# Seven of eight down-projection slices by one level of Strassen's algorithm, in a two-layer decoder step

## The reference, cut to what matters

```
def sqrelu_mlp(h, w_up, w_down):
    return jnp.square(jax.nn.relu(h @ w_up)) @ w_down

x += sqrelu_mlp(rms_norm(x, g), w_up, w_down)      # twice: layer 0 and layer 1
```

## Time and profile before

| | us |
|---|---|
| median of 3 runs | 2395.38 |
| lowest, highest run | 2393.91, 2808.45 |
| span of the profiled execution, first to last instruction | 2393.5 |

### The profile page before, as it was taken

One profiled execution on the slowest core, in us unless ns is written; L12 is line 12 of the kernel. 1 busy time (PEld: TensorE's weight loads), 2 busy tenths in 40 slices (PEclk: granted clock), 3 DMA queues, 4 the chain that ended last, 5 costly groups with the idle time before them and its releaser, 6 DMA issues.

```text
span 2393.5 us, 35212 instructions
## 1 busy us (share of the span) xinstructions
PE 2375.2 (99%) x15165; PEld 2312.2 (97%) x15165; DVE 1002.9 (42%) x1410; ACT 574.3 (24%) x1022; POOL 112.3 (5%) x131
## 2 busy tenths in 40 slices
PE   8999999999999999999999999999999999999999
PEld 8997899999999999999999998889999999999999
DVE  6449724433433333435623325545343333333333
ACT  6549722111111111102310115422111110110111
POOL 1005400000000000000000004100000000000000
PEclk9999999999999999999999999999999999999999
DMA  8621031111111111111321126341111111111112
GB/s 228 87 48 71 11 100 52 38 53 36 53 35 53 38 50 46 42 38 50 100 66 36 36 99 187 126 132 36 53 53 36 53 35 53 35 53 36 52 36 73
DMA packets 134264, 150.30 MB, mean 63 GB/s; under 512 B 33581, under 2 KB 109449, under 8 KB 134012
## 3 DMA queue, kind: packets, MB, share of 16 engines
q1 hardware_dynamic: 131228, 136.11, 19.2%
q0 software_dynamic: 2720, 12.56, 1.6%
q10 hardware_dynamic: 224, 0.30, 0.0%
HBM read 126.50 MB, written 24.47 MB: 63 GB/s over the span
## 4 chain that ended last, share of the span: by engine, by line
PE 96%; ACT 1%; DVE 1%; issue 0%; DMA 0%; DVEq 0%
PE ps L316 42%; PE ps L323 21%; PE ps L300 8%; PE ps L304 7%; PE ps L301 7%; PE ps L551 1%; PE ps L1033 1%; PE ps L1009 1%; PE ps L990 1%; ACT prob L1101 1%; PE ps L2080 1%; PE ps L1410 1%; PE ps L1411 1%; PE ps L1412 1%; PE ps L2061 1%; PE ps L2065 1%
## 5 line engine op out<-in xcount | busy, mean ns | idle before, releaser
L1537 DVE TENSOR_TENSOR x<-x,ps 128x1074 f32<-128x1074 f32 (+1 forms) x126 | 159.3, 1264 | 448.7 <-PE ps L323 448.7
L264 ACT ACTIVATE w_hi<-raw 128x1024 fp32r<-128x1024 f32 x180 | 187.4, 1050 | 648.8 <-PE ps L323 485.6
L316 PE MATMUL ps<-h_hi,w_lo 128*128 128x352 f32 (+2 forms) x1536 | 333.5, 325 | 0.0
L316 PE MATMUL ps<-h_hi,w_hi 128*128 128x352 f32 (+2 forms) x1536 | 333.4, 325 | 0.0
L316 PE MATMUL ps<-act_hi,w_hi 128*128 128x358 f32 (+1 forms) x1512 | 329.5, 326 | 0.0
L316 PE MATMUL ps<-act_hi,w_lo 128*128 128x358 f32 (+1 forms) x1512 | 328.5, 325 | 0.0
L323 PE MATMUL ps<-act_lo,w_hi 128*128 128x358 f32 (+1 forms) x1512 | 269.7, 325 | 0.0
L1519 DVE SCALAR_TENSOR_TENSOR relu<-ps,rstd 128x1074 f32<-128x1074 f32 (+1 forms) x64 | 81.1, 1267 | 447.4 <-PE ps L323 447.4
L316 PEld LDWEIGHTS ps<-h_hi,w_lo 128*128 128x128 f32 x1536 | 263.7, 189 | 0.0
L316 PEld LDWEIGHTS ps<-h_hi,w_hi 128*128 128x128 f32 x1536 | 263.5, 189 | 0.0
L323 PE MATMUL ps<-h_lo,w_hi 128*128 128x352 f32 (+2 forms) x1536 | 263.5, 326 | 0.0
(11 more groups left out here) (339 smaller groups left out, 2419.6 us busy)
## 6 DMA issues: line engine op xcount, KB each, us to landing
raw<-in_mlp_w_up SPq DMA_DIRECT2D x32, 1024.0 KB, 5.5
raw<-in_mlp_w_down SPq DMA_DIRECT2D x32, 1024.0 KB, 5.0
raw<-in_mlstm_w_in SPq DMA_DIRECT2D x12, 1024.0 KB, 5.4
x<-scratch_x SPq DMA_DIRECT2D x8, 537.0 KB, 6.2
scratch_x<-x POOLq DMA_DIRECT2D x1, 4296.0 KB, 14.1
x<-scratch_x SPq DMA_DIRECT2D x8, 528.0 KB, 4.7
x_tok<-in_x_prompt SPq DMA_DIRECT2D x8, 512.0 KB, 7.8
raw<-in_attn_w_qkv SPq DMA_DIRECT2D x16, 256.0 KB, 6.7
```

Of the source, the lines that this page charges most:

```text
L264: nc.scalar.activation(unit_view(w_hi, slot, down), raw_unit(j, rslot, down), ACT.Copy).then_inc(w_hi_ready, 1)
L316: nc.tensor.matmul(ps[:, bank + g, 0:c.stop - c.start], w_block(w, slot, k, kc, cols), hi[:, k, c], start=start and i == 0, stop=False)
L1537: nc.vector.tensor_tensor(view(x[:, o, :]), view(x[:, o, :]), ps[:, out_banks(n):out_banks(n) + 3, 0:w], ALU.add).then_inc(out_free, 1)
```

## The change

The first seven slices of each layer make the down-projection by one level of Strassen's algorithm. The eighth slice keeps the old way. The weights of a slice (512 hidden rows by 1024 outputs) are taken in 4 pairs `p` of output blocks, each pair a 2 x 2 matrix of halves: hidden half `kh` by output half `fh`. The activations of the slice are a 2 x 2 matrix too: hidden half by token half (536 columns, 528 in layer 1). Seven products P1 to P7 of (a weight or a sum of weights) with (an activation or a sum of activations) replace eight. A product has 2 x 2 x 3 = 12 matmuls of 268 (264) columns; 28 products make a slice.

The running sums are made in place: the activations' by `t_pool` and the weights' by `weight_sum_pool`, both on POOL. The partial sums that several outputs share stay in PSUM: chain "a" holds P1, then P1+P6, P1+P6+P5, and P1+P6+P5+P3, and after each step `add_dve` adds the content to one quarter of `x`. A product may only start when the add of the product before it in the chain is done (`earlier` in `product_pe`). 28 adds of 536 columns replace 8 of 1072.

Seven factors of 536 columns for each of two hidden blocks `idx` (14 in all) are split by `factor_hi` (ACT) and `factor_lo` (DVE), where 4 activations were split before. The weights of a product are 256 columns wide and are split by `prod_hi` and `prod_lo` into a ring of 11 slots, which the up blocks' weights share. POOL's order in a slice is: for `idx` 0 the sums t0 to t3; t0 of `idx` 1; the first weight sum; t1 to t3 of `idx` 1; then for each pair the weight sums 1, 2, 3 and sum 0 of the next pair. The up block called 4 in the new code is block 0 of the next slice, made ahead of the products; the last product runs behind the first step of the next up block. Weights come in DMAs of 512 KB instead of 1 MB. The small matrix `head_ones` leaves the first load of constants and comes by a DMA of its own, and several tiles move to other addresses.

```diff
+PRODUCTS = {"P1": (0, 0, 0, "a", True, 0, 0), "P7": (0, 1, 4, "b", True, 1, 1), "P6": (0, 1, 5, "a", False, 1, 0),
+            "P2": (1, 0, 2, "g", True, 0, 0), "P4": (1, 1, 6, "b", False, 1, 0), "P5": (0, 0, 1, "a", False, 1, 1),
+            "P3": (1, 0, 3, "a", False, 0, 1)}
+for _p in range(PAIRS):
+    ORDER += [("P1", _p)] + ([("P3", _p - 1)] if _p else []) + [(_n, _p) for _n in ("P7", "P6", "P2", "P4", "P5")]
+ORDER.append(("P3", PAIRS - 1))
+FACTORS = tuple((idx, f) for idx in range(2) for f in (0, 1, 3, 2, 4, 5, 6))
...
+        def product_pe(pe, layer, i, m):
+            name, p = ORDER[m]
+            _, _, f, chain, start, _, _ = PRODUCTS[name]
+            earlier = {"P6": ("P1", p), "P5": ("P6", p), "P3": ("P5", p), "P4": ("P7", p),
+                       "P7": ("P4", p - 1), "P2": ("P2", p - 1), "P1": ("P3", p - 2)}[name]
+            pe.wait_ge(ring_lo_ready, since("ring_lo_ready", layer, i * EVENTS + (E_M0 + m + 1)))
+            if earlier in M_OF:
+                pe.wait_ge(added, since("added", layer, i * NPROD + (M_OF[earlier] + 1)))
+            if m < 7:
+                pe.wait_ge(fac_lo, since("fac_lo", layer, i * NFAC + (FAC_OF[1, f] + 1)))
+            if m == 0:
+                pe.wait_ge(up_taken, since("up_taken", layer, i * 4 + 4))
+            elif name == "P2" and p == 0:
+                pe.wait_ge(up_taken, since("up_taken", layer, i * 4 + 5))
+            for k in range(2):
+                wh, wl = ring_w(slot_of(m), k)
+                last = block_mms(chain_banks(layer, chain, p), wh, wl, f_hi[:, f, k, :], f_lo[:, f, k, :],
+                                 half_cols(layer) // 2, 2, start and k == 0, k == 1, True)
+            last.then_inc(prod, 1)
...
+        def factor_lo(dve, layer, i, idx, f):
+            h = half_cols(layer)
+            dve.wait_ge(fac_hi, since("fac_hi", layer, i * NFAC + (FAC_OF[idx, f] + 1)))
+            nc.vector.tensor_tensor(f_lo[:, f, idx, 0:h], factor_src(layer, f), f_hi[:, f, idx, 0:h].bitcast(F32),
+                                    ALU.subtract).then_inc(fac_lo, 1)
+        def t_pool(pool, layer, i, idx, n):
+            a1, a2, b1, b2 = quarters(layer)
+            if n == 0:
+                pool.wait_ge(fac_lo, since("fac_lo", layer, split_of(0)))
+                nc.gpsimd.tensor_tensor(a1, a2, a1, ALU.subtract).then_inc(t_made, 1)
+            elif n == 1:
+                pool.wait_ge(act_sqd, since("act_sqd", layer, i * 4 + (2 * idx + 2)))
+                pool.wait_ge(t_made, since("t_made", layer, i * 8 + (4 * idx + 1)))
+                nc.gpsimd.tensor_tensor(a2, b2, a2, ALU.subtract).then_inc(t_made, 1)
...
+        def weight_sum_pool(pool, layer, i, p, n):
...
+            elif n == 1:
+                pool.wait_ge(ring_lo_ready, since("ring_lo_ready", layer, split_of("P7")))
+                nc.gpsimd.tensor_tensor(a21, a22, a21, ALU.subtract).then_inc(w_sum, 1)
...
+        def add_dve(dve, layer, i, m, x):
+            dve.wait_ge(prod, since("prod", layer, i * NPROD + (m + 1)))
...
+            o = x[:, 2 * p + fh, h * th:h * th + h].rearrange("p (g n) -> p g n", g=2)
+            nc.vector.tensor_tensor(o, o, ps[:, b:b + 2, 0:h // 2], ALU.add).then_inc(added, 1)
...
+        def mlp_slice_act(act, layer, i, entry):
...
+            square_act(act, layer, i, 3)
+            for f, m in ((3, None), (2, None), (4, 0), (5, 1), (6, 2)):
+                factor_hi(act, layer, i, 1, f, entry)
+                if m is not None:
+                    prod_hi(act, layer, i, m)
+            for m in range(3, 7):
+                prod_hi(act, layer, i, m)
+
+            square_act(act, layer, i, 4)
+            for m in range(7, NPROD):
+                prod_hi(act, layer, i, m)
...
+        def mlp_slice_dve(dve, layer, i, x, entry):
...
+            relu_dve(dve, layer, i, 3, i * NFAC + 7)
+            for f, m in ((3, None), (2, None), (4, 0), (5, 1), (6, 2)):
+                factor_lo(dve, layer, i, 1, f)
+                if m is not None:
+                    prod_lo(dve, layer, i, m)
+            for m in range(3, 7):
+                prod_lo(dve, layer, i, m)
+
+            relu_dve(dve, layer, i, 4, i * NFAC + NFAC)
+            for m in range(NPROD):
+                if m + 7 < NPROD:
+                    prod_lo(dve, layer, i, m + 7)
+                if m == 22:
+                    ring_unit_lo(dve, layer, 1, ring_hi_ready, ...)
+                add_dve(dve, layer, i, m, x)
```

More of the change, by code:

```diff
@@ L1470, in local_outs @@
[L1470 to L1496, removed]
-                if j < prefetch:
[L1498 to L1502, removed]
+            def load_unit(j, col):
+                sp.dma_start(raw_unit8(j), up[:, :, bass.ds(i * 512 + col, P)]).then_inc(ring_in[RAW_OF[j]], 16)
@@ new lines, in ring_unit_hi, with ring_unit_lo @@
+        def ring_unit_hi(act, layer, i, j, in_count, done):
+            act.wait_ge(ring_in[RAW_OF[j]], since(f"ring_in{RAW_OF[j]}", layer, in_count))
+            for k, hi, lo in unit_parts(j):
+                last = nc.scalar.activation(hi, raw_unit8(j)[:, k, :], ACT.Copy)
+            last.then_inc(done, 1)
+        def ring_unit_lo(dve, layer, j, hi_ready, hi_count, done):
+            dve.wait_ge(hi_ready, hi_count)
+            for k, hi, lo in unit_parts(j):
+                last = nc.vector.tensor_tensor(lo, raw_unit8(j)[:, k, :], hi.bitcast(F32), ALU.subtract)
+            last.then_inc(done, 1)
@@ L1503, in mlp_slice_act @@
                     for o in (2 * j - 8, 2 * j - 7):
-                        act.wait_ge(out_free, i * 12 + (n0 + 5 + o))
+                        act.wait_ge(out_free, n0 + o + 1)
                         if o == 0:
-                            act.wait_ge(act_split, i * 4 + (ups + 4))
+                            act.wait_ge(act_split, ups + 4)
                         norm_act(act, norm[0], o, norm[1], norm[2])
-        def mlp_slice_dve(dve, layer, u0, n0, i, x, prefetch=8, norm=None, takes=None, units=8):
-            ups = 4 * SLICES * layer
-            t, w, view = mlp_cols(layer)
-            r = rstd[:, :, :] if layer == 0 else rstd1()
-            for j in range(units):
-                if j < prefetch:
[L1515 to L1545, removed]
@@ L1563, in first_up_pe @@
                     norm_pe(pe, m, k // 2)
[L1564 to L1575 removed]
+            last.then_inc(up_ready, 1)
@@ new lines, in up_pe, with ring_weights @@
+        def up_pe(pe, layer, j, hi, lo, weights, between=None):
+            _, w, _ = mlp_cols(layer)
+            for k in range(KC):
+                wh, wl = weights(k)
+                last = block_mms(up_banks(layer, j), wh, wl, hi[:, k, :], lo[:, k, :], w, 3, k == 0, k == KC - 1)
+                if k == 0 and between:
+                    between()
+            last.then_inc(up_ready, 1)
+        def ring_weights(j):
+            return lambda k: ring_w(UNIT_SLOTS[j % 4][k // 2], k % 2)
@@ L1592, in mlp_slice_pe @@
+                    for k in range(early, 4):
+                        pe.wait_ge(act_split, ups + k + 1)
+                        pass_hi(slot, k, 4, cols, bank, act_hi, False, w)
+                        last = pass_lo(slot, k, 4, cols, bank, act_lo, True, w)
                     last.then_inc(out_ready, 1)
```

515 lines of the change are left out of this document (439 added, 76 removed).

## The result

The changed kernel takes 2376.26 us in the median of 4 runs (2373.27 to 2379.12), the kernel before 2394.81 beside it: a ratio of 0.9923, with a 95% interval of 0.9911 to 0.9935. One of the four runs before took 2808.45 us and is a slow one; the ratio goes by the fast runs. The change gains 18.5 us, which is within 2%. I had forecast 2344 (own range 2337 to 2356), a gain of 51.

A forecast was written before the change was run, and what follows sets the result against it. PE's matmul rate was taken as the bound: 2393.5 - 14 x (5.87 gain - 2.24 stall) = 2342.7 us of span, with the median 1.9 above it, 2344. Own range 2337 to 2356; with rivals 2320 to 2385.

The forecast's parts named there:

- The price of the matmuls: Down matmuls: 7/8 of the columns, 123.2 ns a matmul; gain 5.87 us a slice, 82.2 us over 14 slices.
- Rival E: Down matmuls: a fixed part per matmul gives 54 us back, median near 2399; chance 0.03.
- The place and the chain: PE idles once a slice, before the third product, released by DVE's add; operations from relu 4 take 4.0 us.
- The size of the stall: Stretch through up block 4: blocking between DVE and POOL makes relu 4 1.2 us late; stall 2.2 us a slice.
- POOL's prices: POOL's sums: 1.23 us at 536 columns and 0.66 at 256, from rows at 512 and 128 columns.
- rival D: Product stretch: DVE becomes the bound at 1.66 us a product, 2415; stalls could lower the clock, 20 us; chance 0.10.
- B: Before product 2: the blocking hardly coincides; stall 1.05 us a slice, median 2328; chance 0.17.
- C: Before product 2: blocked operations pay start-up in full, weight sums precede relu 4; stall 4.1 us, median 2371; chance 0.19.
- The DMAs, the smaller load of constants and PE's waits: Costed at nothing: DMAs at most 5.5 us, asked 8 us ahead; constants about 1 us at most; waits have 0.4 us a product.

The follow-up runs named there:

- the kernel without waits: Against the changed kernel: relu 4 right after product split 2, adds ahead of splits, product splits 9 and 10 both behind product 3's add; 2312.95 us, ratio 0.9658.
- Both experiments on the row: Against the changed kernel, one each: add of product m ahead of split m+7, 2335.71 us; hi copy of product 7 ahead of square 4, 2340.18 us.
- the one on the splits' operand: Against the changed kernel: factor splits read their second operand from PSUM, not SBUF (wrong values), and product 0 waits for all of them; 2330.24 us, ratio 0.9729.
- the kernel with one split more: Against the changed kernel: DVE makes product split m+8 instead of m+7 ahead of the add of product m; 2392.39 us, ratio 0.9989.

## Why the prediction was right or wrong

**The price of the matmuls** was right: they start 0.123 us apart, and the kernel without waits gained 82.2 us. Rival E (a fixed part per matmul) falls: a matmul of 3/4 of the columns takes 3/4 of the time (0.123 against 0.164 us). The figures of the Trainium skill (page "TensorE: Matmul & The Clock Gate", section "Back-to-back issue gap"), about 81 ns at 128 columns and 131 at 512, do not hold for this kernel.

**The place and the chain** were right: idle once a slice, at product 2, released by the add of product 0; from relu 4's start to product 2 are 3.9 us, where the forecast had 4.0 with the 0.13 us before the relu. Both experiments on the row and the one on the splits' operand show it.

**The size of the stall failed.** The steps were "so relu 4 is 1.2 us late" and, from it, "Stall: 2.2 us a slice". Relu 4 was 2.3 us late and the stall 3.37. Blocking was rightly seen as the cause, and its price in this stretch was too low: 2.2 us instead of 1.2. The order of the steps is that of the schedule, and the delay grows along them (ends in us behind up block 3's end, 533.88 in the trace; a step's end is its start and length added):

| step | schedule | trace | late by |
|---|---|---|---|
| t1 starts | 2.58 | 2.76 | 0.18 |
| t2 | 5.48 | 5.89 | 0.41 |
| product split 0 | 8.0 | 8.59 | 0.6 |
| f6 | 9.45 | 10.17 | 0.7 |
| weight sum 1 | 9.98 | 10.78 | 0.8 |
| relu 4 | 14.4 | 15.48 | 1.1 |

Of the 1.13 us by which the stall was too short, 0.57 are POOL's prices: drawn through rows at 512 and 128 columns of other operations, they gave 1.23 us for what took 1.34, and 0.66 for 0.74, and seven such sums lie in the stretch, each holding DVE up. The run with shorter sums shows this part. 0.18 is there before the first sum. Three factor splits that stand behind another split of DVE (f4, f5, f6) were scheduled at 0.55 us from end to end and take 0.63: 542.47 to 543.09 and 543.42 to 544.05 in the rows above. That makes 0.24. The last 0.14 lies in the shorter up block (11.78 us against 11.84) and in hand-overs and roundings, which I did not take apart. The term is 14 x 1.13 = 16 us.

**The clock was priced in the wrong case.** Falls stood under rival D alone, at 1.4 us each, "20 us in all", and not in my forecast, whose range for the stall went to 3.1. They cost some 1.5 us each: a slice of layer 1 without waits is 87.55, with the stall of 3.35 and the 0.1 at its end it would be 91.0, and it is 92.51. Behind the last stall the clock stays down longer:

```profile
2237.27:2242.27 5.00, 5.00 (x22) 5.00 (x23) 2.47 (x5) 1.75 (x5) 2.30 (x4) 0.50 0.34 105
```

The seven are 11 us in the profiled execution: it is 59.8 us longer than that of the kernel without waits (2371.5 and 2311.7), and 14 x (3.36 + 0.1), the waits of 3.21 with 0.15 and 0.1 added, explain 48.4. The median of the runs lies 4.8 above that span instead of 1.9, at lower mean clocks, so about 3 us more. Together 16 for the stall, 1.4 for its end (14 x 0.1), 11 and 3 make 31.4 of the 32 us by which the forecast missed: half of it is the stall, and nearly half the clock.

**The rivals.** B was right on its own condition: with the blocking of the factor splits taken away, 2330 against the 2328 worked out. It failed here because the blocking coincides in every slice. C came nearest, 5 us below the median, but not by its mechanism: its 2371 has a stall of 4.1 (its own 16.1 for the end of relu 4 would make 3.9) and no falls, and relu 4 ended at 15.5. Nor does a blocked split pay its start-up: product split 0 ends 0.29 us after t3 (542.47, 542.18), priced 0.28, where a free one takes 0.41. D's bound in the product stretch did not come: neither the changed kernel nor the one without waits has PE wait at a later product, and in the latter a product keeps its 1.48 us. The DMAs, the smaller load of constants and PE's waits were rightly costed at nothing: the kernel without waits has a span of 2311.7, and 2393.5 - 82.2 is 2311.3. The prediction calls 536 columns half-way between ACT's two rows; they lie a third of the way, which gives the 0.65 us that it states and the trace shows.

## What to carry to other kernels

When an engine that was never the bound gets work in a hand-written order, write the schedule of the fullest stretch and look for the short operation that PE needs and that stands behind long ones: here the order of a few lines of DVE's program was worth 63 us, and the sums of busy time said nothing of it. Schedule with hand-overs and the measured price of each operation in the mode it runs in (free, blocked, or close behind another), since errors add up along the chain, fourteen times over. A stall of PE has a second price, the clock behind it: forecast it in the main case as soon as the stall comes near those after which the clock is seen to fall.

## What the runs showed of the hardware that was not expected

- Whether the granted clock falls behind a stall does not hang on its length alone. In the profiled executions, after waits up to 1.7 us it never fell (five kernels, 14 waits each), after 3.56 always (14). Between, it was mixed: after 2.65 us it fell in 8 of 14, three of them in layer 0, where the other four slices have the same instructions and the same wait; after 3.2 us in all 7 of layer 1 and none of layer 0. This is one execution of each kernel: the other three of the change had a mean clock of 0.990 to 0.991 instead of 0.993 and took 2.7 to 5.9 us longer, so there the clock was down for longer. What tells the stalls apart stays open.
- A fall costs 1.3 to 2.8 us a slice, with 22 to 30 matmuls in the 5 us behind the stall instead of 40: the lower end is the pair of slices shown, the upper one the slice from 555.28 of the kernel with one split more, which took 95.29 us where 88.69, the stall of 3.7 and the 0.1 at its end make 92.5.
- DVE's split and POOL's sum block each other: a factor split of 0.70 us took up to 1.87, and the sum t2 of 1.34 us took 1.83. With one of DVE's inputs in PSUM the split took 0.71 and t2 1.35.
